# Layer 1's memory K and V products spread among layer 0's experts, with three units outside the ring in layer 0

## The reference

```python
h = rms_norm(x, mix_norm); ...            # attention, gated and convolution mixers
x = x + merged @ w_out
m = rms_norm(mem, mem_norm[l])            # mem: 256 x 1024, the same in every layer
kv = m @ w_xkv[l]                         # 1024 -> 2048: K and V of the memory
x = x + cross_attention(rms_norm(x), kv)
x = x + hierarchical_moe(rms_norm(x))     # 32 experts, top 2 of one group of 8
```

## Time and profile before

| | before |
|---|---|
| median of 3 runs | 1767.78 us (1765.42 to 1768.20) |
| profiled execution | 1769.31 us |
| its span | 1767.5 us |
| PE busy | 1372.3 us (78%) |
| DVE busy, ACT busy, POOL busy | 590.3, 450.1, 107.9 us |
| moved by transfers | 534.22 MB, 302 GB/s over the span |
| granted TensorE clock, mean | 0.888 of full speed |

### The profile page before, as it was taken

The page is one execution under the profiler, slowest core; times in us unless marked ns, Lnnn a source line. Parts: engine busy times, 40 slices in busy tenths (PEclk is TensorE's granted clock), DMA queues, the critical chain, the costliest instruction groups (busy, mean ns, idle before and its releaser), DMA issues.

```text
span 1767.5 us, 30850 instructions
## 1 busy us (share of the span) xinstructions
PE 1372.3 (78%) x13372; PEld 1054.9 (60%) x13372; DVE 590.3 (33%) x841; ACT 450.1 (25%) x643; POOL 107.9 (6%) x29
## 2 busy tenths in 40 slices
PE   3989999896986765756666999998977766765765
PEld 3989999886953433423333999998854433433433
DVE  5648756563110101001003587566431100101002
ACT  5444444444310100101003345444330100100101
POOL 3500101003400000000000011010000000000000
PEclk8999999998998987888886999999989888887986
DMA  9552448432699999999999533583289999999993
GB/s 337 179 188 96 143 168 309 154 137 79 227 393 426 427 426 428 426 427 426 428 422 374 179 120 138 197 306 123 96 333 408 427 428 427 426 427 426 421 427 161
DMA packets 92486, 534.22 MB, mean 302 GB/s; under 512 B 9890, under 2 KB 13242, under 8 KB 66108
## 3 DMA queue, kind: packets, MB, share of 16 engines
q1 hardware_dynamic: 83592, 519.14, 72.9%
q10 hardware_dynamic: 8756, 13.01, 2.1%
HBM read 525.84 MB, written 6.29 MB: 301 GB/s over the span
## 4 chain that ended last, share of the span: by engine, by line
PE 46%; DMA 34%; issue 8%; DVE 8%; ACT 2%; ACTq 1%; POOL 0%; SPq 0%; POOLq 0%; DVEq 0%
DMA ring<-in_w_expert_out 33%; PE banks L1338 22%; PE banks L1674 6%; PE banks L1365 5%; PE banks L1623 4%; PE banks L1637 3%; PE banks L1685 2%; DVE hT L880 1%; DVE m_lo L893 1%; DVE arena L1204 1%; PE banks L1499 1%; DMA arena<-in_final_norm 1%; DVE arena L1237 1%; PE banks L1515 1%; DVE stat L877 0%
## 5 line engine op out<-in xcount | busy, mean ns | idle before, releaser
L1623 PE MATMUL banks<-ring,arena 128*32 128x256 f32 x4064 | 293.8, 442 | 133.2 <-DMA ring<-in_w_expert_in 126.3
L1623 PEld LDWEIGHTS banks<-ring,arena 128*32 128x32 f32 x4064 | 136.5, 123 | 271.3 <-DMA ring<-in_w_expert_in 161.7
L1338 PE MATMUL banks<-h_hi,w_hi 128*128 128x256 f32 x848 | 243.5, 287 | 5.1 <-DVEq L838 5.1
L1338 PE MATMUL banks<-h_hi,w_lo 128*128 128x256 f32 x848 | 241.0, 284 | 0.0
L848 DVE TENSOR_TENSOR w_lo<-ring,w_hi 128x2048 fp32r<-128x2048 f32 (+1 forms) x90 | 185.0, 2055 | 146.7 <-ACTq L514 137.2
L1674 PE MATMUL banks<-ring,arena 128*32 128x256 f32 x2048 | 160.3, 466 | 93.0 <-DMA ring<-in_w_expert_out 77.8
L527 ACT CAST w_hi<-ring 128x2048 fp32r<-128x2048 f32 (+1 forms) x114 | 196.8, 1727 | 92.8 <-PE banks L1338 39.8
L1199 DVE TENSOR_TENSOR arena<-arena,banks 128x128 f32<-128x128 f32 x65 | 18.8, 289 | 597.6 <-ACT arena L805 597.6
L1338 PE MATMUL banks<-h_lo,w_hi 128*128 128x256 f32 x720 | 204.9, 285 | 0.0
L805 ACT ACTIVATE arena<-banks 128x128 f32<-128x128 f32 x65 | 18.1, 278 | 714.7 <-PE banks L1623 714.7
L497 POOL TENSOR_TENSOR w_lo<-ring,w_hi 128x2048 fp32r<-128x2048 f32 (+1 forms) x24 | 107.5, 4490 | 1071.8 <-ACTq L514 1071.8
(11 more groups left out here) (289 smaller groups left out, 1953.6 us busy)
## 6 DMA issues: line engine op xcount, KB each, us to landing
ring<-in_w_expert_in SPq DMA_DIRECT2D x127, 2048.0 KB, 23.6
ring<-in_w_expert_out SPq DMA_DIRECT2D x64, 2048.0 KB, 24.8
ring<-in_w_in SPq DMA_DIRECT2D x24, 2048.0 KB, 8.3
ring<-in_w_xkv SPq DMA_DIRECT2D x8, 2048.0 KB, 12.4
ring<-in_w_branch SPq DMA_DIRECT2D x12, 1024.0 KB, 5.1
ring<-in_w_out SPq DMA_DIRECT2D x4, 2048.0 KB, 8.2
ring<-in_w_xq SPq DMA_DIRECT2D x4, 2048.0 KB, 10.8
ring<-in_w_xo SPq DMA_DIRECT2D x4, 2048.0 KB, 8.5
```

The source lines that it names most:

```text
L1338: ins = pe.matmul(acc, stationary(a, k), moving(b, k), start=k == 0 and n == 0, stop=k == kc - 1 and n == 2)
L1623: ins = pe.matmul(G[32 * j:32 * j + 32, :], xTe[:, k, e * SL:(e + 1) * SL], w[:, k % 4, :, j * P:(j + 1) * P], start=k == 0, stop=k == KC - 1,
```

## The change

- The four units `xk0`, `xk1`, `xv0`, `xv1` of layer 1 are taken out of the ring. Each is loaded into `spare_unit` after unit 6 of the experts has left it: the first behind expert unit 15, the others behind units 36, 54 and 72 (`KV_LOAD_BEHIND`), once PE has finished the unit before it. The fetch of the normalised memory is issued by SP just ahead of the first.
- ACT and DVE make the parts of the memory after expert 6, and split both halves of a unit after experts 7, 13, 19 and 25 (`KV_CAST_IN`). DVE subtracts in place, in `spare_unit`; POOL has no part in layer 1's K and V any more.
- PE runs the eight pieces in experts 8, 9, 14, 15, 20, 21, 26 and 27 (`KV_PIECE_IN`), one to an expert, between the transposes and the second product. All eight sums use PSUM bank 6, which a gather and two small jobs give up for it.
- ACT copies each sum into half of `lnt` and stores it by itself: eight transfers of 256 KB in place of two of 1 MB.
- Layer 0's experts are written out on all engines instead of three turns in a loop.
- `SPARE` becomes `(3, 3)`: units 7 and 8 of layer 0's experts are loaded as in layer 1.
- `ysb`, the copy of the second product's sum, moves from the arena to `stat`.

The core of the diff:

```diff
-SPARE = (1, 3)
+SPARE = (3, 3)
-        names += [(layer + 1, n) for n in KV_UNITS if layer + 1 < L]
+        pieces += [(layer + 1, n, h) for n in KV_UNITS if layer + 1 < L for h in range(2)]
+KV_LOAD_BEHIND = (15, 36, 54, 72)
+KV_CAST_IN = (7, 13, 19, 25)
+KV_PIECE_IN = (8, 9, 14, 15, 20, 21, 26, 27)
...
-                for name in KV_UNITS if layer + 1 < L else []:
-                    load_dense(layer + 1, name)
...
+                def next_kv_load(j):
+
+                    name = KV_UNITS[j]
+                    if j:
+                        sp.wait_ge(S["acc_ready"], piece_job(layer + 1, KV_UNITS[j - 1], 1)[1])
+                    else:
+                        sp.wait_ge(S["mhat_stored"], 16)
+                        sp.dma_start(next_mhat.rearrange("p a b -> p (a b)"), mhat_dram).then_inc(S["mhat_loaded"], 16)
+                    sp.dma_start(spare_unit[:, :].rearrange("p (k n) -> p k n", k=KC), source(layer + 1, name)).then_inc(S["next_kv_loaded"], 16)
+
+                if layer + 1 < L:
+                    for n in range(head + R, 3 * NE):
+                        ring_unit(n)
+                        if n in KV_LOAD_BEHIND:
+                            next_kv_load(KV_LOAD_BEHIND.index(n))
...
-                if layer + 1 < L:
-                    make_k(layer + 1, router_exps)
-                    make_v(layer + 1)
-                else:
-                    router_exps()
+                router_exps()
+
+                def next_kv(n):
+
+                    if n == KV_CAST_IN[0] - 1:
+                        act.wait_ge(S["mhat_loaded"], 16)
+                        act.wait_ge(S["units_used"], 3 * NE * layer + R + 3)
+                        memory_high(layer + 1, next_mhat, next_hi)
+                    if n in KV_CAST_IN:
+                        split_to(layer + 1, KV_UNITS[KV_CAST_IN.index(n)], 1, ahead=0)
+                    if n in KV_PIECE_IN:
+                        i = KV_PIECE_IN.index(n)
+                        kind, i = i // 4, i % 4
+                        stage = lnt[:, i % 2, :]
+                        stored = S[f"stage_stored{i % 2}"]
+                        if kind or i >= 2:
+                            act.wait_ge(stored, 16 * (2 * kind + i // 2))
+                        evac(layer + 1, ("xk", "xv")[kind], i, two(stage), "kv_made")
...
-                for i in range(2) if layer + 1 < L else []:
-                    dense(layer + 1, f"xk{i}", "xk", m, i0=2 * i, waits=m_part(layer + 1) if i == 0 else None)
-                for i in range(2) if layer + 1 < L else []:
-                    dense_tokens(layer + 1, f"xv{i}", "xv", m, i0=2 * i)
...
+                def next_kv(n):
+
+                    if n in KV_PIECE_IN:
+                        i = KV_PIECE_IN.index(n)
+                        pe.wait_ge(S["m_ready"], KC * (layer + 2))
+                        if i < 4:
+                            dense(layer + 1, f"xk{i // 2}", "xk", (next_hi, next_lo), i0=i - i % 2, halves=(i % 2,))
+                        else:
+                            dense_tokens(layer + 1, f"xv{i // 2 - 2}", "xv", (next_hi, next_lo), i0=i - i % 2 - 4, halves=(i % 2,))
...
                         ins.then_inc(Q["swt_turned"], 1)
+                        between(e)
                         pe.wait_ge(Q["hidT_ready"], n0 + (e + 1))
```

More of the change, by code:

```diff
@@ L342, in by_pool @@
             layer, unit, half = piece
-            return unit[:2] in ("xk", "xv") or unit == "br00" or (unit, half) in (("wo0", 1), ("cc", 1))
+            return layer == 0 and unit[:2] in ("xk", "xv") or unit == "br00" or (unit, half) in (("wo0", 1), ("cc", 1))
         def split_count(n):
@@ L457, in _ @@
                     ring_unit(n)
[L458 to L464, removed]
+                def next_kv_load(j):
[11 more added lines that the diff above has]
+                            next_kv_load(KV_LOAD_BEHIND.index(n))
+                else:
+                    with sp.Fori(0, TURNS - 1) as turn:
+                        for n in range(head + R, head + R + 3 * EI):
+                            _, slot = expert_place(layer, n)
+                            sp.wait_ge(S["units_used"], turn * (3 * EI) + (3 * NE * layer + n - R + 1))
+                            expert_unit(ring[:, slot, :], turn * EI + n // 3, n % 3, slot_loaded[slot])
+                    for n in range(head + R + 3 * EI * (TURNS - 1), 3 * NE):
+                        ring_unit(n)
                 X = extra_sems[layer]
@@ L1369, in dense_by_parts, with dense_tokens @@
                         done(ins)
-            def dense_tokens(layer, unit, job, x, i0=0):
-                for half in range(2):
+            def dense_tokens(layer, unit, job, x, i0=0, halves=(0, 1)):
+                for half in halves:
                     w = piece(layer, unit, half)
@@ L1716, in slot_wait @@
                             pe.wait_ge(slot_loaded[slot], turn * (16 * per) + 16 * (u // R + 1 - (base + 1) * per))
-                    experts(main_sems, turn, EI, slot_wait, unit_done, lambda e, x: unit(e, x, first), count, small_jobs)
-                main_turn(base, (starts, tables))
-                with pe.Fori(base + 1, base + TURNS) as turn:
-                    main_turn(turn)
+                    experts(main_sems, turn, EI, slot_wait, unit_done, lambda e, x: unit(e, x, first), count, small_jobs, between)
+                if layer + 1 < L:
+                    main_turn(base, (starts, tables), next_kv)
+                    for turn in range(1, TURNS):
+                        main_turn(base + turn, between=lambda e: next_kv(turn * EI + e))
+                else:
+                    main_turn(base, (starts, tables))
+                    with pe.Fori(base + 1, base + TURNS) as turn:
+                        main_turn(turn)
                 X = extra_sems[layer]
```

138 lines of the change are left out of this document (84 added, 54 removed).

## The result

| | before | after |
|---|---|---|
| median | 1767.99 us (4 runs) | 1734.65 us (4 runs, 1732.36 to 1738.56) |
| profiled execution, its span | 1769.31, 1767.5 us | 1732.36, 1730.6 us |
| PE, DVE, ACT busy | 1372.3, 590.3, 450.1 us | 1351.1, 606.1, 449.6 us |
| moved by transfers | 534.22 MB, 302 GB/s | 534.15 MB, 309 GB/s |

The ratio is 0.9816 with a 95% interval of 0.980 to 0.983: 33.3 us faster, against the 32 us from 1767.8 to 1736 that were forecast. The same kernel measured again beside later experiments gave 1733.93 us, ratio 0.9808 (0.9793 to 0.9822).

What follows compares the result with a forecast made beforehand. The kernel alternates between PE-bound and transfer-bound stages. 64.8 us won, less 22.8 for units, 2.5 memory, 5 stores and 2 unevenness, gives 32.5 us, a median of about 1736 us; range 1726 to 1753.

Steps and rivals of the forecast that it cites:

- The first gather: Head of layer 0's experts: PE reaches the gather 57.2 us earlier, about 13 us after the last dense piece.
- Unit 23: Third unit of layer 0's expert 7: lands 64.8 us earlier by layer 1's pattern, before added loads.
- The rest of the queue: Layer 0's saturated stretch: added transfers are paid in full, K and V units at 5.7 us each.
- stores: K and V stores, 2.10 MB in eight pieces among layer 0's experts: 5 us, range 0 to 10.
- unevenness: Transfers at the head of layer 0's second turn: the queue never empties, 2 us charged.
- The head of the second turn: Experts 8 and 9 of layer 0, the tightest place: queue never empties, 2 us charged, range 0 to 6.
- PE work hidden: Layer 0's experts: pieces of 5.84 us fit the 6.5 us PE has free per expert.
- Rival 1: Pairs of pieces, mainly experts 8 and 9: queue runs dry at the lower clock, about 1751 us; chance 0.16.
- rival 2: All eight experts with pieces: transfers pay each piece's length, slower at 1781 to 1828 us; chance 0.04.
- rival 3: Layer 0's experts: instruction fetch of written-out code or load-store interference eats 30 us, about 1766 us; chance 0.03.
- Behind it nothing changes: After layer 0's last landing: layer 1's first units follow as before, its experts keep code and order.
- own range: Whole kernel: 1727 to 1746 us from the ranges for stores, units and head of the turn; chance 0.74.

Runs made afterwards that it cites:

- e1_one_spare: Changed kernel with SPARE back at (1, 3), so units 7 and 8 of layer 0's experts go through the ring again; 1743.7 us.
- e8_memory_early: Changed kernel with the 1 MB normalised memory fetched right behind unit 8 of layer 0's experts instead of behind unit 15; 1732.21 us.
- e7_stored_twice: Changed kernel with each of the eight 256 KB stores issued twice, the second to its own place in HBM; 1741.82 us.
- e6_long_rows: Changed kernel with layer 1's four K and V units read from an expert's matrix in 16 KB rows instead of 2 KB, same bytes; 1733.42 us.
- e5_no_products: Changed kernel with 6 in place of 48 matmuls in each of layer 1's K and V pieces; 1734.07 us.
- e4b_pieces_twice: Changed kernel with each of layer 1's eight K and V pieces computed twice and nothing else doubled; 1744.19 us.
- e3_before_written_out: Kernel before the change with layer 0's experts written out on all engines in place of the loop, nothing else; 1771.16 us, ratio 1.0017.
- e4_pieces_twice: Changed kernel with each of the eight pieces computed twice, and layer 1's `vg` doubled as well by the same edit; 1753.53 us.

## Why the prediction was right

- **The first gather, 57.2 us earlier.** Measured 13.1 us from the last dense piece, layer 1's 13.2. Right.
- **Unit 23.** Forecast 64.8 us earlier by layer 1's pattern, less 5.7 and 2.5 for what now stands ahead of it: 56.6, arriving 111.7 us after the last dense piece. Measured 57.2 and 111.1. Right; `e1_one_spare` confirms the part of the two units with 8.8 us, `e8_memory_early` that of the memory with 2.4.
- **The rest of the queue.** Forecast 17.1 for three units, 5 for stores, 2 for unevenness, 24.1 in all; measured 20.9. The stores were right (5.3 for the same bytes in `e7_stored_twice`). That leaves 15.6 us for three units and all unevenness, at most 5.2 each: I had taken the price of rows of 2 KB from two windows at the start of layer 1's dense loads, and among the experts' long rows they cost less. The rule of the Trainium skill that the prediction names ("DMA: Bandwidth & Descriptors", Specifications), line rate from 512 bytes, would give 4.9. The trace agrees with it only roughly: in `e6_long_rows` the same bytes in rows of 16 KB cost 0.5 us less a unit.
- **The head of the second turn.** Charged with 2 us; windows at 428 and 421 GB/s put it at 46 x (1 - 421/427), under 1 us, and with long rows (`e6_long_rows`) the second window has 427. The main reason given held: the pieces ran at 5.74 us, the upper clock. The rest came out by luck. The working set the loss of a 2.90 us wait against 4.6 us of DVE's subtractions, and that wait belongs to the third turn. Against what the second turn really was before, the first issue behind the gather moved from 13.9 to 21.8 us after the landing of unit 23. The forecast had 20.8 us give or take 2 for it, since the third turn had been late by about as much for another reason. The queue covered it either way.
- **PE work hidden.** Right, with `e5_no_products` at no gain and `e4b_pieces_twice` losing 6.7 of its 8 to 10 us where the forecast saw the tightest place. Rival 1's mechanism, a queue run dry at the first pair, thus exists, but it showed only at twice the length; rival 2 is refuted. So is the cost of written-out code in rival 3: `e3_before_written_out` lost 2.5 us, none of them in layer 0, where unit 23 and the last landing keep their distances to 0.2 us.
- **"Behind it nothing changes"** was wrong by 3 us: the issue at the end of layer 1 grew from 1.34 to 4.37 us. From the last landing of layer 0 to the end the kernel takes 822.1 us for 820.4, since 1.1 us less pass before layer 1's last dense piece and 0.3 less in its experts. I had taken writing out the loop for free, since the queue hides the turns; the step failed in not asking what a program of another length does to a branch that the edit leaves alone.

The profiled executions differ by 36.9 us: 57.2 won up to unit 23, less 20.9 in the expert stretch, less 1.7 behind it, and 2.3 ahead of the last dense piece of layer 0 (407.25 and 404.94). These 2.3 are not the change's: that piece ends anywhere from 403.9 to 409.1 in the kernels here. That the sum came out within 2 us is in part luck, since the queue cost 3 us less than charged and the wait at the end 3 us more.

The own range was also added up wrongly by 2 us: with the lowest price of every term its lower end is 1725 and not 1727, which changes nothing in the judgement. Three parts of the change were not run by themselves: the stores in eight pieces in place of two, `ysb` in `stat`, and POOL's share of the subtractions moved to DVE. The account above leaves no more than a few us to them together.

## What to carry to other kernels

Where a kernel alternates between stages bound by an engine and stages bound by transfers, work of the engine moved into the second kind can be free as long as the queue of loads outlasts it (here 5.7 us at a time against five outstanding loads of 5 us), and its own transfers are paid by their bytes. Price such a move at one landing in the saturated stretch, not at the start of the stage, and count as won only the time in which transfers had been idle. Place the work away from points where the engine is already late. When reading rows at the head of a turn, check which turn it is, since the first pass into a loop and its later ones wait differently. When a result is off by a few us, compare the branches far from the edit too.

## What was not expected of the hardware

- The wait at a branch over unused code was 1.24 to 1.34 us in six kernels and 4.31 to 4.67 us in seven. Two of them, `e4_pieces_twice` and `e4b_pieces_twice`, differ only in 96 matmuls far ahead of it. Edits of a few matmuls can move it, and 3 us is more than `e8_memory_early` was meant to win.
- The hardware loop on PE cost 5.3 us without work at its two branches back in layer 0 (third and fourth turn) and nothing on the way in (second turn).
- Behind a 2 MB load in rows of 2 KB the next issue on the same queue took 4.17 to 12.96 us; in rows of 16 KB, 0.33 us. At the last three of the four units the transfers kept 420 GB/s or more.
- The 2 KB rows cost 0.5 us on 2 MB among the experts' loads. That is what the window of 386 GB/s would give (2.10 MB in 5.4 us for 4.9) and half of what the one of 348 GB/s would (6.0 us).
